# Bias tables of the dilated heads loaded in ten pieces, and four maxima scaled on another engine

## The reference, cut to what matters

```python
out_a = mixer_dilated(heads(q_a), heads(k_a), heads(v_a), rel_bias)        # 8 heads of 64
out_b = mixer_mla(c_q, c_kv, k_rope, g_q_latent, w_q_up, g_kv_latent, w_kv_up)  # 8 latent heads

def dilated_window_attention(q, k, v, rel_bias, dilation, half_steps):
    ...
    bias = rel_bias[t5_relative_bucket(rel_steps * dilation)]
    scores = where(valid, q @ k.T * dh ** -0.5 + bias, NEG_INF)
    m = max(scores); p = exp(scores - m); l = sum(p)
    ...                      # (window, dilation) = (128, 1), (512, 4), (2048, 16), merged by their weights
```

## Time and profile before

| what | from | value |
|---|---|---|
| median of the timed runs | times | 4206.54 us |
| profiled execution, span | times, page | 4209.23 us, 4207.1 us |
| granted TensorE clock, mean | page | 0.949 |
| busy over the span | page | PE 89%, DVE 50%, ACT 46%, POOL 31% |
| front stage | timeline | 0 to 290.3 us |
| PE busy, 110 to 262 us | windows | 129.48 of 152.00 us, clock 0.92 |
| start of the attention stage, 290 to 316 us | windows | PE 8.38, DVE 12.92, ACT 11.19, POOL 15.93 of 26.00 us; DMA share 1.01 |
| attention stage, 316 to 660 us | windows | PE 336.19, DVE 293.69, ACT 236.39, POOL 207.56 of 344.00 us |
| first latent scores of successive head pairs | timeline | 362.21, 406.71, 451.25 us: a period of 44.5 us |

### The profile page before, as it was taken

One profiled execution on the slowest core, in us unless ns is written; L12 is line 12 of the kernel. 1 busy time (PEld: TensorE's weight loads), 2 busy tenths in 40 slices (PEclk: granted clock), 3 DMA queues, 4 the chain that ended last, 5 costly groups with the idle time before them and its releaser, 6 DMA issues. The chain is left out here.

```text
span 4207.1 us, 54618 instructions
## 1 busy us (share of the span) xinstructions
PE 3764.7 (89%) x20181; PEld 3154.6 (75%) x20181; DVE 2084.0 (50%) x3842; ACT 1924.7 (46%) x3526; POOL 1296.1 (31%) x779
## 2 busy tenths in 40 slices
PE   8879997869977999999498875897999999999998
PEld 6658886757746777887388874797888768888886
DVE  4228884277745333221566657674234227433453
ACT  5126675347746455422365654564324234323331
POOL 0016660000003223311133333122632103876541
PEclk9989998879988999999799997998999999999999
DMA  3663434489957222321322212113653112222542
GB/s 123 174 166 84 97 85 136 162 331 421 422 221 231 80 80 87 97 92 68 88 60 80 81 54 79 61 32 127 227 157 116 65 51 90 91 86 85 191 149 96
DMA packets 399770, 549.36 MB, mean 131 GB/s; under 512 B 178660, under 2 KB 272740, under 8 KB 390541
## 3 DMA queue, kind: packets, MB, share of 16 engines
q1 hardware_dynamic: 381580, 479.75, 35.5%
q10 hardware_dynamic: 10720, 39.85, 2.4%
q0 software_dynamic: 7200, 26.22, 1.6%
HBM read 402.48 MB, written 147.43 MB: 131 GB/s over the span
## 5 line engine op out<-in xcount | busy, mean ns | idle before, releaser
L3291 POOL TENSOR_TENSOR mid_w_lo<-mid_w_raw,mid_w_hi 128x1024 fp32r<-128x1024 f32 (+1 forms) x64 | 153.8, 2408 | 405.9 <-ACT mid_w_hi L3479 405.9
L4025 POOL TENSOR_TENSOR end_w_lo<-end_w_raw,end_w_hi 128x1024 fp32r<-128x1024 f32 x60 | 147.3, 2464 | 334.3 <-ACT end_w_hi L4367 334.1
L3649 PE MATMUL mid_ps<-mid_w_hi,mid_xT_hi 128*128 128x512 f32 x576 | 229.2, 398 | 1.9 <-DVE mid_xT_lo L3353 1.9
L3649 PE MATMUL mid_ps<-mid_w_hi,mid_xT_lo 128*128 128x512 f32 x576 | 225.0, 391 | 0.0
L3649 PE MATMUL mid_ps<-mid_w_lo,mid_xT_hi 128*128 128x512 f32 x576 | 224.9, 390 | 0.0
L4683 PE MATMUL end_ps<-end_w_hi,end_xT_hi 128*128 128x512 f32 x544 | 214.4, 394 | 0.0
L4683 PE MATMUL end_ps<-end_w_hi,end_xT_lo 128*128 128x512 f32 x544 | 212.1, 390 | 0.0
L4683 PE MATMUL end_ps<-end_w_lo,end_xT_hi 128*128 128x512 f32 x544 | 211.7, 389 | 0.0
L1478 DVE SCALAR_TENSOR_TENSOR moe_w_lo<-moe_wgu,moe_gcol,moe_w_hi 128x512 fp32r<-128x512 f32 x272 | 185.5, 745 | 7.7 <-ACT moe_w_hi L1618 7.7
L1439 POOL DMA_INDIRECT moe_xb<-xrows,moe_idx x34 | 32.1, 944 | 468.0 <-PE moe_x_ps L40 273.1
L1618 ACT ACTIVATE moe_w_hi<-moe_wgu,moe_gcol 128x512 fp32r<-128x512 f32 x272 | 173.2, 716 | 2.9 <-DMA moe_wgu<-in_w_gate_up 2.9
(11 more groups left out here) (678 smaller groups left out, 11525.1 us busy)
## 6 DMA issues: line engine op xcount, KB each, us to landing
moe_wgu<-in_w_gate_up SPq DMA_DIRECT2D x34, 2048.0 KB, 12.0
moe_wd<-in_w_down SPq DMA_DIRECT2D x34, 1024.0 KB, 14.6
mid_w_raw<-in_w_in SPq DMA_DIRECT2D x60, 512.0 KB, 4.1
end_w_raw<-in_w_ffn_out SPq DMA_DIRECT2D x44, 512.0 KB, 3.8
end_w_raw<-in_w_ffn_in SPq DMA_DIRECT2D x40, 512.0 KB, 4.4
expert_rows<-moe_out ACTq DMA_DIRECT2D x34, 512.0 KB, 11.3
in_tail<-mid_y SPq DMA_DIRECT2D x56, 256.0 KB, 2.1
qkvT<-mid_conv SPq DMA_DIRECT2D x24, 512.0 KB, 4.4
```

What stands on the lines that cost most here:

```text
L3291: pool.tensor_tensor(w_lo[:, c % 2, 2 * q:2 * q + 2, 0:wid], w_raw[:, 2 * q:2 * q + 2, 0:wid], w_hi[:, c % 2, 2 * q:2 * q + 2, 0:wid].bitc ...
L3649: ins = pe.matmul(o_, lhsT, rhs, start=(k == 0 and part == 0), stop=(k == KC - 1 and part == 2))
L4025: pool.tensor_tensor(halves(w_lo, piece), w_raw[:, 2 * q:2 * q + 2], halves(w_hi, piece).bitcast(F32), ALU.subtract).then_inc(w_split, 1)
```

## The change

The front stage no longer expands the tables: `expand_table`, the tile `never`, the DRAM tensor `tables` and two semaphores go, and `table_step` ends one position earlier. The attention stage builds each table in SBUF from `skew` by ten DMAs instead of one; the masked parts, the same for all heads, are set once by four GpSimd memsets in both buffers, and the first table's DMAs wait for these (`pads_set`, now 9). The product with minus the scale moves from VectorE to ScalarE, which waits for it itself (`negated`); VectorE signals each of the four maxima. The first job splits q before k, and PE scores the segments in the order 2, 3, 0, 1 and waits for `q_near` only ahead of segment 0.

```diff
+    topped_by = exped_by
+    TABLE_LOADS = 6 + STRIDE
+    PADS = 9
@@ load_table
                     if i >= 2:
-                        sp.wait_ge(topped, last_unit[j - 4] + 1)
-                    sp.dma_start(table[:, i % 2], jobs[j]["bias"]).then_inc(table_in[i % 2], 16)
+                        sp.wait_ge(topped, topped_by[last_unit[j - 4]])
+                    elif i == 0:
+                        sp.wait_ge(pads_set, PADS)
+                    view = table[:, i % 2, 0:3 * SEG].rearrange("p (w b c u) -> p w b c u", w=3, b=2, u=BLOCK)
+                    first, second, far = jobs[j]["bias"]
+                    for w in range(2):
+                        sp.dma_start(view[:, w + 1, 0], first).then_inc(table_in[i % 2], 16)
+                        sp.dma_start(view[:, w, 1], second).then_inc(table_in[i % 2], 16)
+                    sp.dma_start(view[:, 0, 0, :, EDGE:], first[:, :, EDGE:]).then_inc(table_in[i % 2], 16)
+                    sp.dma_start(view[:, 2, 1, :, 0:EDGE], second[:, :, 0:EDGE]).then_inc(table_in[i % 2], 16)
+                    for c in range(STRIDE):
+                        sp.dma_start(table[c * BLOCK:(c + 1) * BLOCK, i % 2, 3 * SEG:], far[c]).then_inc(table_in[i % 2], 16)
@@ PE, score
-                        if sparse[j]:
-                            pe.wait_ge(near_q, rank[j] + 1)
...
-                        for g in range(SEGS):
+                        for g in (2, 3, 0, 1):
                             i = 2 * t + g % 2
+                            if t == 0 and g == 0:
+                                pe.wait_ge(near_q, rank[j] + 1)
@@ ScalarE
-                act.wait_ge(k_in[0], 32)
-                act.activation(k_hi[:, 0, EDGE:EDGE + T], kT[:, 0], ACT.Copy).then_inc(first_hi, 1)
                 act.wait_ge(q_in[0], 32)
                 act.activation(q_hi[:, 0], qT[:, 0], ACT.Copy).then_inc(first_hi, 1)
+                act.wait_ge(k_in[0], 32)
+                act.activation(k_hi[:, 0, EDGE:EDGE + T], kT[:, 0], ACT.Copy).then_inc(first_hi, 1)
...
                         if sparse[j]:
+                            tops = keep[:, rank[j] % 2, 0:2, 2 * t:2 * t + 2, DV]
+                            act.activation(neg_top[:, n % 4].rearrange("p (k s) -> p k s", k=2), tops, ACT.Copy, scale=-job["scale"]).then_inc(negated, 1)
+                            act.wait_ge(negated, sparse_by[n])
@@ VectorE, tops_sparse
-                    dve.memset(pad[:], 0.0)
+                    ch.wait()
+                    ch.add(dve.memset(pad[:], 0.0))
...
-                        ch.add(dve.tensor_tensor_reduce(biased[:, n % 2, here], s_ps[:, n % 2, here], table[:, i, at:at + SEG],
-                                                        1.0, -3e38, ALU.add, ALU.max, keep[:, i, g // 2, w, DV:DV + 1]))
-                    ch.wait()
-                    dve.tensor_tensor(neg_top[:, n % 4].rearrange("p (k s) -> p k s", k=2), keep[:, i, 0:2, 2 * t:2 * t + 2, DV],
-                                      minus[:].rearrange("p (k s) -> p k s", k=2), ALU.mult).then_inc(topped, 1)
+                        dve.tensor_tensor_reduce(biased[:, n % 2, here], s_ps[:, n % 2, here], table[:, i, at:at + SEG],
+                                                        1.0, -3e38, ALU.add, ALU.max, keep[:, i, g // 2, w, DV:DV + 1]).then_inc(topped, 1)
@@ GpSimd, start of the stage
                 pool.memset(v_near[:], 0.0).then_inc(pads_set, 1)
+                for i in range(2):
+                    view = table[:, i, 0:3 * SEG].rearrange("p (w b c u) -> p w b c u", w=3, b=2, u=BLOCK)
+                    pool.memset(view[:, 0, 0, :, 0:EDGE], NEVER).then_inc(pads_set, 1)
+                    pool.memset(view[:, 2, 1, :, EDGE:], NEVER).then_inc(pads_set, 1)
@@ front stage, table_step
                         else:
                             sp.wait_ge(rows_out, 16 * STRIDE * h)
-                            expand_table(h - 1)
-                        if h == A_HEADS:
-                            return
                         sp.dma_start(raw[:, 0:BIAS], bias_rows[h].partition_broadcast(P)).then_inc(rows_in, 16)
...
-                    if 4 <= p <= 4 + 2 * A_HEADS:
+                    if 4 <= p < 4 + 2 * A_HEADS:
                         table_step(p - 4)
@@ build_program
+    def tables(h):
+        rows, width, pitch = P // STRIDE, BIAS - 1, STRIDE * NEAR
+        def block(ahead):
+            at = (STRIDE - 1) * NEAR + rows - 1 + ahead
+            flat = skew[h, at:at + P * width].rearrange("(p w) -> p w", w=width)
+            return flat[:, 0:pitch].rearrange("p (c z) -> p c z", z=NEAR)[:, :, 0:rows]
+        def far(c):
+            at = c * (rows * width + NEAR - rows) + (2 * STRIDE - 1) * NEAR + P - 1
+            return skew[h, at:at + rows * width].rearrange("(p w) -> p w", w=width)[:, 0:3 * P]
+        return block(0), block(rows), [far(c) for c in range(STRIDE)]
```

More of the change, by code:

```diff
@@ L499, in attend_both @@
         k_hi, k_lo = (st.sb(n, [P, 2, KEYS], F32R) for n in ("k_hi", "k_lo"))
-        one, nought, minus = st.sb("one", [P, 1]), st.sb("nought", [P, 1]), st.sb("minus", [P, SEGS])
+        one, nought = st.sb("one", [P, 1]), st.sb("nought", [P, 1])
         vv, v_near = st.sb("v", [P, 2, NT, DV]), st.sb("v_near", [P, CHUNKS, DV])
@@ L2553, with front_layers @@
 FRONT_PLAN = ("l", "v", "q", "k")
-def front_layers(nc, name, a, ident_dram, v_rows, qkT, lat_v, lat_qkT, bias_rows, skew, tables):
+def front_layers(nc, name, a, ident_dram, v_rows, qkT, lat_v, lat_qkT, bias_rows, skew):
     NT, KC = T // P, D // P
@@ L2673, in store_values @@
                     sp.dma_start(lat_v[t * P:(t + 1) * P, :].rearrange("p (h d) -> p h d", d=B_DIM), vs).then_inc(v_stored, 16)
-                def expand_table(h):
-                    rows, width, pitch = P // STRIDE, BIAS - 1, STRIDE * NEAR
-                    windows = tables[h, :, 0:6 * P].rearrange("p (w b c u) -> p w b c u", w=3, b=2, u=rows)
-                    at = (STRIDE - 1) * NEAR + rows - 1
-                    first, second = (skew[h, s:s + P * width].rearrange("(p w) -> p w", w=width)[:, 0:pitch].rearrange("p (c z) -> p c z", z=NEAR)[:, :, 0:rows]
-                                     for s in (at, at + rows))
-                    for w in range(2):
-                        sp.dma_start(windows[:, w + 1, 0], first).then_inc(tables_out, 16)
-                        sp.dma_start(windows[:, w, 1], second).then_inc(tables_out, 16)
-                    sp.dma_start(windows[:, 0, 0, :, rows // 2:], first[:, :, rows // 2:]).then_inc(tables_out, 16)
-                    sp.dma_start(windows[:, 2, 1, :, 0:rows // 2], second[:, :, 0:rows // 2]).then_inc(tables_out, 16)
-                    sp.dma_start(windows[:, 0, 0, :, 0:rows // 2], never[:]).then_inc(tables_out, 16)
-                    sp.dma_start(windows[:, 2, 1, :, rows // 2:], never[:]).then_inc(tables_out, 16)
-                    for c in range(STRIDE):
-                        s = c * (rows * width + NEAR - rows) + (2 * STRIDE - 1) * NEAR + P - 1
-                        far = skew[h, s:s + rows * width].rearrange("(p w) -> p w", w=width)[:, 0:3 * P]
-                        sp.dma_start(tables[h, c * rows:(c + 1) * rows, 6 * P:], far).then_inc(tables_out, 16)
                 def table_step(m):
@@ L4758, in build_program @@
     bias_rows, skew = dram("bias_rows", (A_HEADS, BIAS)), dram("skew", (A_HEADS, skew_size))
-    tables = dram("tables", (A_HEADS, P, 9 * P))
-    front_layers(nc, "front", a, ident, v_a, qkT_a, v_b, qkT_b, bias_rows, skew, tables)
+    front_layers(nc, "front", a, ident, v_a, qkT_a, v_b, qkT_b, bias_rows, skew)
     mixed, near = dram("mixed", (T, AW + B_HEADS * B_DIM)), dram("near", (A_HEADS, T, A_DIM + 2))
+    def tables(h):
[8 more added lines that the diff above has]
+        return block(0), block(rows), [far(c) for c in range(STRIDE)]
     def by_class_out(columns):
@@ L4767, in build_program @@
                     v=v_a[:, h * A_DIM:(h + 1) * A_DIM], out=by_class_out(slice(h * A_DIM, (h + 1) * A_DIM)),
-                    scale=A_DIM ** -0.5, bias=tables[h], near=near[h]) for h in range(A_HEADS)]
+                    scale=A_DIM ** -0.5, bias=tables(h), near=near[h]) for h in range(A_HEADS)]
     latent = [dict(depth=NOPE + ROPE, dv=B_DIM, q=qkT_b[h], k=qkT_b[B_HEADS + h], v=v_b[:, h * B_DIM:(h + 1) * B_DIM],
```

28 lines of the change are left out of this document (10 added, 18 removed).

## The result

| | kernel before | changed kernel |
|---|---|---|
| median (range, runs), same chip | 4209.12 us (4204.45 to 4213.43, 4) | 4180.12 us (4178.12 to 4187.47, 4) |
| the same again on another chip | 4207.2 us (4199.6 to 4219.02, 11) | 4182.7 us (4173.79 to 4185.81, 6) |
| profiled execution, span | 4209.23, 4207.1 us | 4180.7, 4178.6 us |
| granted TensorE clock, mean | 0.949 | 0.951 |

The ratio is 0.9934, with a 95% interval of 0.9917 to 0.9952: faster by 0.66%, some 28 us. Again on the other chip it was 0.9939 (0.9926 to 0.9953). The forecast was 4180.0.

A forecast was written before the change was run, and what follows sets the result against it. The prediction took front-stage PE stalls behind stores late in SyncE's queue as the removable bound; -31 + 6.6 - 2 = -26.4 us gave 4182.8 from the profiled execution, 4180.1 from the median; forecast 4180, range 4171 to 4196.

The forecast's parts named there:

- What bounds the kernel: Front stage: PE idle 22.5 us, waiting on ScalarE's copies, held by head stores late in SyncE's queue.
- Part 1: Front stage: the expansion leaves SyncE's queue, some 62 us of issues; PE's stalls go, -31 us.
- the upper bound: Front stage: at most 33.7 us gained, six up-projection periods taking 132.0 us instead of 165.7.
- Part 2: Attention stage's start: the first table's ten issues delay the values and the latent queries and keys, +6.6 us.
- Nothing more for the clock, as PE stood before this point too: Attention stage's start: the longer PE gap adds no slow-clock cost beyond the +6.6 us.
- Part 3: Later heads' tables: ten issues each, 5.9 us more of SyncE, covered by 7.2 us of waiting; cost 0.
- Rival E: Attention stage: issues into SBUF back up, deciding from 1.5 us each; slower, +64 us, 4271; chance 0.06.
- Part 4: Dilated attention units: the four maxima scaled on ScalarE instead of VectorE, -2 us.
- The cap: Dilated heads: the first latent unit waits for GpSimd's keys, so at most 0.3 us a head in 7 heads.
- B: Front stage: head stores stay late through the DMA engines, not their issue; gain only 18, 4193; chance 0.14.
- C: Attention stage: ScalarE becomes the bound of the dilated units, +7.7 us, 4190; chance 0.08.
- D: Front stage: something beside SyncE sets the pace, the gain is given back, +5, 4211; chance 0.06.

The follow-up runs named there:

- values first: Changed kernel with the first head's value loads issued ahead of its ten table DMAs: 4175.73 us, ratio 0.991.
- the scaling alone: Kernel before with only the scaling of the four maxima moved from VectorE to ScalarE: 4207.9 us, ratio 0.9993.
- the GpSimd expansion with scaling: Kernel before with the table expansion issued by GpSimd instead of SyncE and the four maxima scaled on ScalarE: 4174.2 us, ratio 0.9917.

## Why the prediction was right, step by step

**What bounds the kernel.** Right, and shown: PE waited for SyncE's issues, through a store and a copy. Moving the same issues to another queue gives 32.1 to 33.5 of the 33.9 us, and the traffic is worth the rest.

**Part 1, -31.** The stage ended 31.23 us sooner. Inside that two things cancel: the stretch from the first to the last up-projection gave 33.94, the whole of the upper bound and a little more, so the 3 us that I took off for thin margins weren't there; and the first up-projection came 2.77 us later (103.79 with 101.02). That isn't the change's: over all profiles it falls between 100.5 and 105.5 us, with both kinds of kernel. The pieces were sized well: in windows of 1 us of the kernel before, from 101 to 267 us, PE was idle for 24.7 us and lost 8.3 more to the clock while busy, 33.0 together, where I had 22.5 and 7.

**Part 2, +6.6.** The place and the direction were right, values first shows it, and the sum of the start is near (+7.7 in the profiled execution). Its terms were not. The ten issues took 5.25 us, not 6.5, and the last value piece went out 5.55 us later, not 6.9. Then I let it land as late behind its issue as before. It had landed 4.0 us after it, and now took 1.8, so the split came 16.05 us after the start and not 19: 5.55 - 2.2 = +3.3. All eight profiles with one load of 576 KB for the first table have that landing at 3.3 to 4.3 us, all five with ten loads, in either order, at 1.8 to 2.0. That large load was itself 6.9 us on the way; why the pieces behind it are slower, no run isolates.

The step that failed is "Nothing more for the clock, as PE stood before this point too": the longer gap was followed by 13 us at half clock, +4.4 in this execution, against nothing in another of the same kernel (45.29 with 45.26). Beside the 0.55 us of a shorter period that is +5.0 and +0.6. So the start costs 3 to 8 us, and in the first execution the sum was right by two errors that cancel, which is luck. The gap of 7.66 us is near the forecast of 8 to 9 by luck too: 2.2 of it come from PE being done sooner, which I had set down as no gain and no cost.

**Part 3, 0.** Right. The loads of a later table went out in SyncE's idle time. SyncE's queue of the changed kernel in a steady head, one with a slow issue:

```profile
335.20 0.59 SPq L579 DMA_DIRECT2D att_table<-skew  x1
...
337.48 1.69 SPq L581 DMA_DIRECT2D att_table<-skew  x1
...
339.77 1.90 SPq L584 DMA_DIRECT2D att_table<-skew  x4
...
344.75 0.45 SPq L601 DMA_DIRECT2D att_v_near<-v_a  x1
```

Ten issues take 6.5 us here, 0.65 each, and the scaling alone, with one issue a table, has the same period of 43.97. Rival E's sign is there, and not only here: the fifth issue of a table is slow in most heads, and the ten take 6.5 to 7.9 us in the later ones and 9.9 in the second, 0.99 each. E needed 1.5 on average.

```profile
L581 SPq DMA_DIRECT2D att_table<-skew x8: 507/1788/4283, 267.2 to 557.4; - x8
```

The Trainium skill (DMA: Bandwidth & Descriptors, Specifications) says that pieces under 512 B cost a read-modify-write, by which the first table would have landed late. The trace doesn't show that: the table's pieces landed 1.8 to 2.6 us after their issue, all by 271.9, which is 12.8 us after the stage's start and not 15.5. Later ones took up to 7.5 us (L579, with a median of 4.9), where the earlier trace rows had 2.5 to 3.8; but the one load of 576 KB, in long rows, had taken 6.0 to 11.7 (L572).

**Part 4, -2.** Right in sign and place, too small: 0.55 us a head instead of 0.3, -3.6 with the tail. The cap was read wrongly. I had the first latent unit wait for GpSimd's keys already in the kernel before. They were ready at 406.43, and PE came to them at 406.71 straight from its last weighted values, with no idle time. Its waits at these scores (us, times, longest) from 305 to 665 us before, and from 255 to 650 us of the changed kernel:

```profile
PE att_s L669 <- issue: 2.1, 1, 2.1
...
PE att_s L681 <- issue: 8.8, 7, 7.7
```

Before, only the wait of the start is there; six more come with the change. So PE's own way through the dilated units was the longer one, and the keys are what it meets now. They come sooner themselves: GpSimd's chain is untouched, but not its beginning, as the merge waits for VectorE's `share` behind the four dilated units, each of which got shorter. From one pair's latent scores to the next merge it was 32.30 us and is 31.92; from the merge to the scores 12.20 and 12.01, as PE no longer comes late. ScalarE's copy took 0.203 us as I took it from L767, beside GpSimd too.

**The rivals.** B, C and D are out: the window with the traffic at full clock, the period, and the front's end. E's mechanism is there, at two thirds of what it needed in the worst head. What is open: what holds a head pair at 43.9 us, now that the keys are level with it, and why the GpSimd expansion with scaling is 8.5 us below the changed kernel by the medians, where their profiles reach the attention stage's end at 639.6 and 640.5 us. These two profiles are of the slowest execution of the one (4177.65 us) and of the fastest of the other (4173.79), so they are no fair pair. No run isolates either.

## What to carry to other kernels

When a queue of issues stands in front of something that PE waits for, count the issues, not the bytes: the same 96 DMAs cost 34 us on the queue that also stores and 0.4 to 1.9 us on one that nobody needs. When issues move to the head of a stage, put what the longest chain waits for (here the values) in front of what has time (the table). And where a small VectorE instruction has a mean far above its shortest (754 ns against 161), look for a GpSimd instruction that ends with it, and change its form or its engine before its place.

## What the runs showed of the hardware that I had not expected

- A 128x4 product on VectorE ran 161 to 1692 ns beside GpSimd as a two-operand one and 170 to 1696 ns with one operand, but 141 to 156 ns when cut into 128x1 pieces, and 193 to 213 ns on ScalarE.
- The slow clock behind a gap of PE isn't set by the gap's length: 0 and 1.7 us lost behind 2.11 us, and 6.6, 1.9 and 2.9 behind 7.66, 7.92 and 8.05. Filling the gap took it to 0.0 in both profiles that tried, as it was in one of the eleven without.
- The last of seven small value loads landed 3.3 to 4.3 us after its issue where one 576 KB load went out ahead of them, and 1.8 to 2.0 where ten smaller ones stood in its place.
- GpSimd's queue took 0.74 us for an issue that SyncE's took 0.64 for, and it didn't matter, as GpSimd had nothing else to do there.
